# Fifteen of sixteen expert pairs written out, and a loop for the last pair and the overflow

## The chip, the core and the metric

The kernel runs on one core of a Trainium2 chip. A core has five engines, each with its own instruction queue: TensorE (PE, matmuls; its weight loads are shown apart as PEld), VectorE (DVE), ScalarE (ACT), GpSimd (POOL) and SyncE (SP), which here only issues DMAs. Engines wait for each other through semaphores. The metric is the time of one execution on the device in microseconds. The kernel before takes 1500.24 us (median of three runs, 1499.53 to 1501.92).

## What is computed

Two layers of a decoder trunk over 256 positions of width 1024, all in float32. Each layer mixes tokens in three branches and then sends each position through two of 32 experts:

```python
for l in range(DEPTH):                       # DEPTH = 2
    h = rms_norm(x, norm_mix_g[l])
    x = x + token_mixers(h, ...)             # "mixing": one wide projection, three branches, gates, w_out
    h = rms_norm(x, norm_ffn_g[l])
    x = x + hier_moe(h, ...)                 # group (argmax of 4), then top 2 of the 8 experts inside it
return rms_norm(x, norm_final_g)

def expert_block(tok_b, e):                  # inside hier_moe, for the rows of one expert
    xb = xt[tok_b]
    hid = silu(xb @ w_gate[e]) * (xb @ w_up[e])
    return hid @ w_down[e]                   # 1024 -> 512 -> 1024, then weighted and added back to x
```

An expert has three matrices of 2 MB. All 32 are read in each layer, whatever the routing says: 201 MB a layer.

## The kernel before

**Stages.** A layer is a mixing stage (its weights come through a ring of buffers and are split into a high and a low part by ACT and DVE), a short routing stage and an expert stage. The code of both layers is written out in Python, so each layer has its own instructions.

**Expert stage.** Experts are taken two at a time, a pair: experts 2i and 2i+1, each with up to 64 rows (`BLK`), fill the 128 rows of a tile. `MAIN_PAIRS` is 16. An expert with more than 64 rows continues in overflow pairs that follow the sixteen; there can be up to four (`MAX_PAIRS` 20). With these inputs there is none: each layer runs 16 pairs. The number of pairs up to the end of each layer is computed on DVE (L1098 to L1105) and written to `pairs_i`; each queue waits for semaphore `pairs_known` and reads it into a register.

**Weights.** `ring` has 12 slots of 1 MB. A pair uses all twelve: slots 0 to 3 for the first halves of gate and up (two experts each), 4 to 7 for their second halves, 8 to 11 for down. SP's `load_pair` issues them in that order; before each two slots it waits for `pair_freed`, which PE raises after each of the six stages of the pair before (four of `gate_up`, L1455, two of `down`, L1467). The loads of the next layer's mixing weights stand behind them in SP's queue.

**One pair g.** PE's `pair` (L1485) does, in this order: `gate_up` 0; adding rows back for the pair before (`scatter`, L1481/L1482) in two parts around `gate_up` 1; transposes of the selection matrix (L1496, L1498); `gate_up` 2 and 3; `gather(0)` (L1443), the first half of the row gather for pair g+1; transposes of `hid` (L1509), which wait for DVE; `gather(1)`; `down` 0 and 1, which wait for ACT's copy of the transposed `hid` (L735). ACT copies the selection (L730, L731), computes silu (L733), copies `hidT` (L735) and the high part of y (L738). DVE adds rows to x (`add_rows`, L1118), builds the selection of the next pair (`choose`, L1087, L1089), multiplies silu by up (L1128), scales the gathered rows of the next pair (`gathered`, L1111) and computes the low part of y (L1132).

**Start of a stage.** DVE chooses the rows of pair 0, computes the pair count, copies the gathered rows, chooses for pair 1, computes `overflow_tables` (L1139 to L1158) and then finishes pair 0 with L1128. PE gathers for pair 0, reads the pair count, runs pair 0 and then loops over the others. The last trip of the loop also gathers, for a pair that may not exist.

Of the kernel before, what the change touches and what calls it, by code (L numbers as in the profile page):

```python
# [29 lines left out]
P = 128  # L30
ALU = mybir.AluOpType
ACT = mybir.ActivationFunctionType
AX = mybir.AxisListType
# [17 lines left out]
def build_trunk(nc, x_in, positions, norm_mix_g, norm_ffn_g, norm_final_g, w_in, gmlp_ws, gmlp_b, conv_w,  # L51
                w_proj_a, w_proj_b, w_proj_c, w_out, router_group_w, router_group_b,
                router_expert_w, router_expert_b, expert_w_gate, expert_w_up, expert_w_down, out):
    _, S, D = x_in.shape
# [15 lines left out]
    BLK = 64  # L70
# [71 lines left out]
    with ExitStack() as ctx:  # L142
# [265 lines left out]
        def alone(eng):  # L408

            eng.sem_inc(passed)  # L410
# [17 lines left out]
        def sync_program(sp):  # L428
# [6 lines left out]
            for l in range(DEPTH):  # L435

                if_known = l * 1 + 1
                sp.wait_ge(pairs_known, if_known)
                alone(sp)
                done = sp.value_load(pairs_i[0:1, bass.ds(l, 1)], min_val=0, max_val=DEPTH * MAX_PAIRS)  # L440
# [66 lines left out]
                end = sp.value_load(pairs_i[0:1, bass.ds(l + 1, 1)], min_val=MAIN_PAIRS, max_val=DEPTH * MAX_PAIRS)  # L507
# [63 lines left out]
        def scalar_program(act):  # L571
# [168 lines left out]
            act.wait_ge(pairs_known, DEPTH + 1)  # L740
            last = act.value_load(pairs_i[0:1, DEPTH:DEPTH + 1], min_val=MAIN_PAIRS, max_val=DEPTH * MAX_PAIRS)
            sqrt_table()
            act.wait_ge(x_added, last * 2)
# [5 lines left out]
        def vector_program(dve):  # L749
# [48 lines left out]
            for l in range(DEPTH):  # L798
# [283 lines left out]
                def choose(i, g):  # L1082
# [14 lines left out]
                nb = S // BLK - 1  # L1097
                link(v.tensor_tensor(beyond[:, :, :], psD[:, 0, 2 * NE:3 * NE].unsqueeze(2).to_broadcast([P, NE, nb]),  # L1098
                                     thresholds[:, :].unsqueeze(1).to_broadcast([P, NE, nb]), ALU.is_gt))
                link(v.tensor_reduce(cumA[:, 16:], beyond[:, :, :], AX.X, ALU.add))  # L1100
                link(v.tensor_reduce(total[:, :], cumA[:, 16:], AX.X, ALU.add))
# [93 lines left out]
        def tensor_program(pe):  # L1195
# [6 lines left out]
            for l in range(DEPTH):  # L1202
# [321 lines left out]
                with pe.Fori(done + 1, end) as g:  # L1524
                    pair(g, False)
# [46 lines left out]
```

## Time and profile before

| | |
|---|---|
| median of 3 runs | 1500.24 us (1499.53 to 1501.92) |
| the profiled execution | 1495.47 us |
| its span, first to last instruction | 1493.7 us |
| PE busy | 1421.6 us, 95% |
| DVE busy | 557.0 us, 37% |
| ACT busy | 423.5 us, 28% |
| weight loads (queue q1) | 488.20 MB, 81.6% of 16 DMA engines' span |
| instruction queues q8 and q14 | 27 and 12 packets, 0.44 and 0.10 MB |
| mean granted clock of TensorE | 0.983 |

A slice of the span is 37.3 us. The mixing stages take about 0 to 265 and 745 to 1003 us, the expert stages 276 to 747 and 1014 to 1485 us. Busy time alone does not tell what bounds: PE is counted busy while a matmul is in the array, and in the expert stages the weight stream is as full as PE is. Times of pieces come from this one profiled execution.

### The profile page before, as it was taken

The page shows a single profiled execution, that of the slowest core. Times are in us where ns is not written, and L with a number is a line of the kernel's source. Part 1 is how long each engine was busy: PE and PEld are TensorE (multiplying, and loading weights), DVE is VectorE, ACT ScalarE, POOL GpSimd, SP SyncE. Part 2 cuts the span into 40 slices and gives each one's busy share as a digit, 9 for nine tenths or more (in the row PEclk, how much of TensorE's full clock was granted, in tenths as well). Part 3 has the DMA queues.
Part 4 walks back from the last instruction along what each step waited for, and adds up shares of the span by engine and source line. Part 5 has one row for each costly group of instructions (what it writes and reads, how often), then busy time and mean ns, then how long its engine had stood idle before and what let it go on. Part 6 is the DMA issues. An engine that isn't in the chain of part 4 may idle for free.

```text
span 1493.7 us, 19746 instructions
## 1 busy us (share of the span) xinstructions
PE 1421.6 (95%) x7463; PEld 859.2 (58%) x7463; DVE 557.0 (37%) x871; ACT 423.5 (28%) x530; POOL 7.5 (0%) x43
## 2 busy tenths in 40 slices
PE   6999999899999999999989999998999999999996
PEld 5899788544444444444478988874444444444443
DVE  6786355522222222212277844654222222222123
ACT  5544332312212212111254543431221221221121
POOL 1000000000000000000000000000000000000000
PEclk9999899899999999999989999998999999999999
DMA  7544364899999999999945443748999999999995
GB/s 271 184 162 169 127 214 165 328 416 422 422 422 422 422 421 422 422 422 423 408 172 177 149 165 137 253 153 359 420 422 422 422 422 422 422 422 422 421 422 229
DMA packets 100799, 489.08 MB, mean 327 GB/s; under 512 B 8686, under 2 KB 12054, under 8 KB 51608
## 3 DMA queue, kind: packets, MB, share of 16 engines
q1 hardware_dynamic: 99656, 488.20, 81.6%
q8 instruction: 27, 0.44, 0.1%
q10 hardware_dynamic: 1104, 0.34, 0.1%
q14 instruction: 12, 0.10, 0.0%
HBM read 487.46 MB, written 1.05 MB: 327 GB/s over the span
## 4 chain that ended last, share of the span: by engine, by line
PE 65%; DMA 24%; DVE 8%; issue 2%; ACT 1%; SPq 0%; POOL 0%; DVEq 0%; ACTq 0%; POOLq 0%
DMA ring<-in_expert_w_up_dram 24%; PE psB L1455 19%; PE psA L1219 14%; PE psB L1219 11%; PE psC L1467 8%; PE psA L1443 5%; DVE ring_parts L814 2%; PE psA L1481 2%; PE psA L1482 1%; DVE work L909 1%; DVE top L908 1%; PE psD L1509 1%; PE psC L1341 1%; PE psC L1340 1%; PE psC L1424 1%
## 5 line engine op out<-in xcount | busy, mean ns | idle before, releaser
L1455 PE MATMUL psB<-ring,share 128*64 128x512 f32 x2048 | 462.5, 596 | 17.9 <-DMA ring<-in_expert_w_up_dram 17.9
L1455 PEld LDWEIGHTS psB<-ring,share 128*64 128x64 f32 x2048 | 142.0, 137 | 290.5 <-issue 270.7
L1467 PE MATMUL psC<-ring,share 128*64 128x512 f32 x1024 | 226.8, 595 | 0.0
L814 DVE TENSOR_TENSOR ring_parts<-ring,ring_parts 128x2048 fp32r<-128x2048 f32 (+1 forms) x80 | 176.7, 2248 | 64.7 <-ACT ring_parts L637 64.4
L637 ACT ACTIVATE ring_parts<-ring 128x2048 fp32r<-128x2048 f32 (+1 forms) x80 | 146.9, 1878 | 57.9 <-PE psA L1219 38.3
L1118 DVE TENSOR_TENSOR x<-x,psA 128x1024 f32<-128x1024 f32 x62 | 75.7, 1221 | 191.4 <-PE psA L1482 191.4
L1467 PEld LDWEIGHTS psC<-ring,share 128*64 128x64 f32 x1024 | 70.8, 137 | 131.7 <-issue 127.8
L1443 PEld LDWEIGHTS psA<-gates,xn 128*128 128x128 f32 x1088 | 130.1, 196 | 27.7 <-issue 26.0
L1443 PE MATMUL psA<-gates,xn 128*128 128x128 f32 x1088 | 139.0, 282 | 1.6 <-DVE gates L1087 1.6
L1219 PE MATMUL psA<-ring_parts,hT_parts 128*128 128x512 f32 (+1 forms) x448 | 134.8, 383 | 2.0 <-DVE ring_parts L847 2.0
L1132 DVE TENSOR_TENSOR gates_parts<-psC,gates_parts 128x512 fp32r<-128x512 f32 x64 | 41.2, 685 | 222.8 <-ACT gates_parts L738 222.8
L1219 PE MATMUL psB<-ring_parts,hT_parts 128*128 128x512 f32 x384 | 121.6, 398 | 0.0
L738 ACT ACTIVATE gates_parts<-psC 128x512 fp32r<-128x512 f32 x64 | 34.7, 595 | 262.9 <-PE psC L1467 262.9
L1219 PE MATMUL psA<-ring_parts 128*128 128x512 f32 (+2 forms) x320 | 109.2, 341 | 0.0
L1219 PE MATMUL psB<-ring_parts 128*128 128x512 f32 (+1 forms) x288 | 99.7, 346 | 0.0
L1128 DVE SCALAR_TENSOR_TENSOR share<-gates,psB 128x512 f32<-128x512 f32 x32 | 23.9, 747 | 197.5 <-PE psB L1455 197.0
L1219 PEld LDWEIGHTS psA<-ring_parts,hT_parts 128*128 128x128 f32 x448 | 83.7, 191 | 17.3 <-issue 2.7
L1219 PEld LDWEIGHTS psB<-ring_parts,hT_parts 128*128 128x128 f32 x384 | 73.4, 193 | 16.2 <-issue 1.1
L1111 DVE TENSOR_TENSOR share<-psA,g_ffn 128x512 f32<-128x512 f32 x68 | 47.0, 691 | 94.7 <-PE psA L1443 94.7
L730 ACT ACTIVATE gates<-psD 64x1 f32<-64x1 f32 x64 | 10.6, 165 | 247.8 <-PE psD L1498 247.4
L735 ACT ACTIVATE share<-psD 128x512 f32<-128x512 f32 x32 | 19.1, 597 | 189.8 <-PE psD L1509 189.8
L1219 PEld LDWEIGHTS psA<-ring_parts 128*128 128x128 f32 x320 | 61.3, 192 | 6.2
(313 smaller groups left out, 1237.3 us busy)
## 6 DMA issues: line engine op xcount, KB each, us to landing
ring<-in_expert_w_gate_dram SPq DMA_DIRECT2D x128, 1024.0 KB, 19.9
ring<-in_expert_w_up_dram SPq DMA_DIRECT2D x128, 1024.0 KB, 20.9
ring<-in_expert_w_down_dram SPq DMA_DIRECT2D x128, 1024.0 KB, 19.5
ring<-in_w_in_dram SPq DMA_DIRECT2D x56, 1024.0 KB, 7.1
ring<-in_w_out_dram SPq DMA_DIRECT2D x8, 1024.0 KB, 5.2
ring<-in_w_proj_a_dram SPq DMA_DIRECT2D x4, 1024.0 KB, 6.2
ring<-in_w_proj_b_dram SPq DMA_DIRECT2D x4, 1024.0 KB, 6.2
ring<-in_w_proj_c_dram SPq DMA_DIRECT2D x4, 1024.0 KB, 6.2
```

What stands on the lines that cost most here:

```text
L637: sc.activation(high_and_low(p)[0], mix_slot(p), ACT.Copy).then_inc(high_act, 1)
L738: sc.activation(y_high[:, n, :], psC[:, n, :], ACT.Copy).then_inc(y_act, 1)
L814: v.tensor_tensor(low_part, mix_slot(p), high_part, ALU.subtract).then_inc(low_dve, 1)
L1111: v.tensor_tensor(xT[:, 4 * b:4 * b + 4, :], psA[:, b, :].rearrange("p (c n) -> p c n", c=4), g_ffn[:, 4 * b:4 * b + 4].unsqueeze(2).to_br ...
L1118: v.tensor_tensor(x[:, t, :].rearrange("p (b n) -> p b n", b=2), x[:, t, :].rearrange("p (b n) -> p b n", b=2), (psB if last and t else ps ...
L1128: v.scalar_tensor_tensor(hid, silu, slot_w, psB[:, 1, :], ALU.mult, ALU.mult).then_inc(hid_done, 1)
L1132: v.tensor_tensor(y_low[:, n, :], psC[:, n, :], y_high[:, n, :], ALU.subtract).then_inc(y_dve, 1)
L1219: ins = te.matmul(o, first, second, start=start and i == 0, stop=stop and i == len(TERMS) - 1)
L1443: ins = te.matmul(psA[:, b, (c % 4) * P:(c % 4 + 1) * P], xn[:, o:o + P], sel[:, t].rearrange("p j n -> p (j n)"), start=t == 0, stop=t == ...
L1455: ins = te.matmul(psB[j * BLK:(j + 1) * BLK, o, :], xT[:, 4 * half + c, j * BLK:(j + 1) * BLK], w[:, c, :], start=half == 0 and c == 0, st ...
L1467: ins = te.matmul(psC[j * BLK:(j + 1) * BLK, n, :], hidT[:, 2 * k + c, j * BLK:(j + 1) * BLK], w[:, c, n * 512:(n + 1) * 512], start=k == ...
L1481: te.matmul(ps[:, n, :], selT[:, t, :], y_high[:, n, :], start=True, stop=False)
```

## The change

Per engine:

- PE: fifteen pairs are written out. Each gathers for the next, except the last of the fifteen (pair 14). Then PE reads the pair count, and a loop covers pair 15 and any overflow pair; each trip gathers its own rows first, both halves, and then runs `pair` without a gather.
- DVE: the same fifteen are written out. The seven instructions of the pair count (`pair_count`) move from before the first `gathered` to after `choose_next(0)`, in front of `overflow_tables`. In the loop a trip copies its own gathered rows, adds the rows of the pair before, chooses for the next and finishes its pair.
- ACT: fifteen trips written out, then the count is read and a loop covers the rest.
- SP keeps its loop. All four queues no longer read the count at the head of a layer: layer 0 counts from the constant 0, layer 1 from the register that holds the end of layer 0.

The arithmetic, the weight loads and their order stay the same. The diff, cut to its core:

```diff
@@ SP, head of a layer
-                if_known = l * 1 + 1
-                sp.wait_ge(pairs_known, if_known)
-                alone(sp)
-                done = sp.value_load(pairs_i[0:1, bass.ds(l, 1)], min_val=0, max_val=DEPTH * MAX_PAIRS)
+                done = end if l else 0
@@ ACT
-                act.wait_ge(pairs_known, l + 1)
-                alone(act)
-                start = act.value_load(pairs_i[0:1, bass.ds(l, 1)], min_val=0, max_val=DEPTH * MAX_PAIRS)
+                start = end if l else 0
...
-                act.wait_ge(pairs_known, l + 2)
-                alone(act)
-                end = act.value_load(pairs_i[0:1, bass.ds(l + 1, 1)], min_val=MAIN_PAIRS, max_val=DEPTH * MAX_PAIRS)
-                with act.Fori(start, end) as g:
+                def pair(g):
...
+                for i in range(MAIN_PAIRS - 1):
+                    pair(start + i)
+                act.wait_ge(pairs_known, l + 2)
+                alone(act)
+                end = act.value_load(pairs_i[0:1, bass.ds(l + 1, 1)], min_val=(l + 1) * MAIN_PAIRS, max_val=(l + 1) * MAX_PAIRS)
+                with act.Fori(start + MAIN_PAIRS - 1, end) as g:
+                    pair(g)
@@ DVE
-                dve.wait_ge(pairs_known, l + 1)
-                alone(dve)
-                start = dve.value_load(pairs_i[0:1, bass.ds(l, 1)], min_val=0, max_val=DEPTH * MAX_PAIRS)
+                start = end if l else 0
...
-                nb = S // BLK - 1
-                link(v.tensor_tensor(beyond[:, :, :], psD[:, 0, 2 * NE:3 * NE].unsqueeze(2).to_broadcast([P, NE, nb]),
...
-                v.tensor_copy(pairs_i[:, bass.ds(l + 1, 1)], pairs_f[:, :]).then_inc(pairs_known, 1)
...
-                        dve.wait_ge(gather_ps, (g + l) * 2 + b + 1)
+                        dve.wait_ge(gather_ps, g * 2 + b + 1)
...
-                def pair_rest(g):
+                def pair_rest(g, gather_next):
...
-                    gathered(g + 1)
+                    if gather_next:
+                        gathered(g + 1)
...
-                gathered(start)
-                choose_next(0, start)
-                overflow_tables()
-                pair_rest(start)
-                with dve.Fori(0, nc.s_assert_within(end - start - 1, MAIN_PAIRS - 1, MAX_PAIRS - 1)) as i:
-
-                    add_rows(start + i)
-                    choose_next(i + 1, start + i + 1)
-                    pair_rest(start + i + 1)
+                gathered(start)
+                choose_next(0, start)
+                pair_count()
+                overflow_tables()
+                pair_rest(start, True)
+                for i in range(1, MAIN_PAIRS - 1):
+                    add_rows(start + i - 1)
+                    choose_next(i, start + i)
+                    pair_rest(start + i, i < MAIN_PAIRS - 2)
+                dve.wait_ge(pairs_known, l + 2)
+                alone(dve)
+                end = dve.value_load(pairs_i[0:1, bass.ds(l + 1, 1)], min_val=(l + 1) * MAIN_PAIRS, max_val=(l + 1) * MAX_PAIRS)
+                with dve.Fori(0, nc.s_assert_within(end - start - (MAIN_PAIRS - 1), 1, MAX_PAIRS - MAIN_PAIRS + 1)) as i:
+
+                    gathered(start + i + MAIN_PAIRS - 1)
+                    add_rows(start + i + MAIN_PAIRS - 2)
+                    choose_next(i + MAIN_PAIRS - 1, start + i + MAIN_PAIRS - 1)
+                    pair_rest(start + i + MAIN_PAIRS - 1, False)
@@ PE
-                pe.wait_ge(pairs_known, l + 1)
-                alone(pe)
-                done = pe.value_load(pairs_i[0:1, bass.ds(l, 1)], min_val=0, max_val=DEPTH * MAX_PAIRS)
+                done = end if l else 0
...
-                    pe.wait_ge(sel_ready, g + l + 2)
-                    pe.wait_ge(x_added, g * 2 + 1)
-                    gather(0)
+                    if gather_next:
+                        pe.wait_ge(sel_ready, g + l + 2)
+                        pe.wait_ge(x_added, g * 2 + 1)
+                        gather(0)
...
-                    gather(1)
+                    if gather_next:
+                        gather(1)
...
+                for i in range(MAIN_PAIRS - 1):
+                    pair(done + i, i == 0, i < MAIN_PAIRS - 2)
...
-                pair(done, True)
-                with pe.Fori(done + 1, end) as g:
-                    pair(g, False)
+                end = pe.value_load(pairs_i[0:1, bass.ds(l + 1, 1)], min_val=(l + 1) * MAIN_PAIRS, max_val=(l + 1) * MAX_PAIRS)
+                with pe.Fori(done + MAIN_PAIRS - 1, end) as g:
+
+                    pe.wait_ge(sel_ready, g + l + 1)
+                    pe.wait_ge(x_added, g * 2 - 1)
+                    gather(0)
+                    gather(1)
+                    pair(g, False, False)
```

## Rows read from the trace of the kernel before

**Rows 1.** The page: busy totals, and GB/s moved in 40 slices of the span.

```profile
PE 1421.6 (95%) x7463; PEld 859.2 (58%) x7463; DVE 557.0 (37%) x871; ACT 423.5 (28%) x530; POOL 7.5 (0%) x43
...
GB/s 271 184 162 169 127 214 165 328 416 422 422 422 422 422 421 422 422 422 423 408 172 177 149 165 137 253 153 359 420 422 422 422 422 422 422 422 422 421 422 229
```

**Rows 2.** Chain in order of time (start us, us, what): pair 1, PE.

```profile
308.75 3.43 PE psB L1455 x16
313.31 3.58 PE psB L1455 x16
318.58 7.02 PE psB L1455 x32
```

**Rows 3.** The same chain, the end of the first layer's expert stage.

```profile
702.14 25.39 DMA ring<-in_expert_w_up_dram
...
727.66 3.65 PE psB L1455 x16
731.32 1.98 PE psA L1443 x16
733.30 0.48 PE psD L1509 x4
733.78 1.79 PE psA L1443 x16
735.57 7.04 PE psC L1467 x32
```

**Rows 4.** ACT reads the count (ns min/median/max, starts); first table load after it.

```profile
L586 ACTq TENSOR_LOAD <-pairs_i x2: 275/380/486, 7.1 to 742.9; - x2
...
7.85 1.28 ACT L581 ACT_TABLE_LOAD   x1 [0.49 <-issue]
```

**Rows 5.** Timeline of pair 0 (start us, us, engine, line; in brackets idle time before).

```profile
276.00 0.25 DVE L1098 TENSOR_TENSOR ycT<-psD,thresholds 128x96 f32<-128x96 f32 x1
277.44 0.15 DVE L1105 CAST pairs_i<-pairs_f 128x1 int32<-128x1 f32 x1
...
279.89 0.69 DVE L1111 TENSOR_TENSOR share<-psA,g_ffn 128x512 f32<-128x512 f32 x1 [2.29 <-PE psA L1443]
...
297.69 0.49 DVE L1158 TENSOR_REDUCE ycT<-rel 128x10 f32<-128x320 f32 x1
298.40 0.75 DVE L1128 SCALAR_TENSOR_TENSOR share<-gates,psB 128x512 f32<-128x512 f32 x1 [0.22 <-DVE ycT L1158]
299.20 0.75 PE L1509 MATMUL psD<-ident,share 128*128 128x128 f32 x4 [0.76 <-DVE share L1128]
299.99 0.60 ACT L735 ACTIVATE share<-psD 128x512 f32<-128x512 f32 x1 [6.31 <-PE psD L1509]
```

**Rows 6.** SP's down loads; windows; landings of loads issued 304.5 to 307, 284 to 287.

```profile
305.49 4.27 SPq L446 DMA_DIRECT2D ring<-in_expert_w_down_dram  x4
...
307.00:308.00 1.00, 1.00 (x8) 0.30 (x6) 0.00 (x0) 0.00 (x0) 0.00 (x0) 1.00 0.87 336
308.00:309.00 1.00, 1.00 (x6) 0.29 (x4) 0.00 (x0) 0.20 (x1) 0.00 (x0) 1.00 1.01 369
309.00:310.00 1.00, 1.00 (x8) 0.42 (x6) 0.57 (x1) 0.98 (x3) 0.00 (x0) 1.00 0.92 385
...
ring<-in_expert_w_down_dram SPq DMA_DIRECT2D x2, 1024.0 KB, 7.8
...
ring<-in_expert_w_gate_dram SPq DMA_DIRECT2D x2, 1024.0 KB, 6.1
```

**Rows 7.** PE from 400 to 700 us; instruction packets of the span, of 310:500, of 295:298.

```profile
400.00:700.00 300.00, 292.15 (x1503) 132.50 (x1501) 64.39 (x93) 58.18 (x95) 0.00 (x0) 1.00 1.01 422
...
q8 instruction: 27, 0.44, 0.1%
...
q8 instruction: 1, 0.02, 0.0%
...
q8 instruction: 1, 0.02, 2.1%
```

More of the change, by code:

```diff
@@ L506, in sync_program @@
                 alone(sp)
-                end = sp.value_load(pairs_i[0:1, bass.ds(l + 1, 1)], min_val=MAIN_PAIRS, max_val=DEPTH * MAX_PAIRS)
+                end = sp.value_load(pairs_i[0:1, bass.ds(l + 1, 1)], min_val=(l + 1) * MAIN_PAIRS, max_val=(l + 1) * MAX_PAIRS)
                 with sp.If(end > done + MAIN_PAIRS):
@@ L738, in scalar_program @@
                         sc.activation(y_high[:, n, :], psC[:, n, :], ACT.Copy).then_inc(y_act, 1)
-            act.wait_ge(pairs_known, DEPTH + 1)
-            last = act.value_load(pairs_i[0:1, DEPTH:DEPTH + 1], min_val=MAIN_PAIRS, max_val=DEPTH * MAX_PAIRS)
+                for i in range(MAIN_PAIRS - 1):
[5 more added lines that the diff above has]
+                    pair(g)
             sqrt_table()
-            act.wait_ge(x_added, last * 2)
+            act.wait_ge(x_added, end * 2)
             sc.activation(xn[:, 0:D], x[:, 0, :], ACT.Square, accum_out=ss[:, 0:1]).then_inc(ss_act, 1)
@@ L1132, in pair_rest, with pair_count @@
                         v.tensor_tensor(y_low[:, n, :], psC[:, n, :], y_high[:, n, :], ALU.subtract).then_inc(y_dve, 1)
+                def pair_count():
+                    nb = S // BLK - 1
+                    link(v.tensor_tensor(beyond[:, :, :], psD[:, 0, 2 * NE:3 * NE].unsqueeze(2).to_broadcast([P, NE, nb]),
+                                         thresholds[:, :].unsqueeze(1).to_broadcast([P, NE, nb]), ALU.is_gt))
+                    link(v.tensor_reduce(cumA[:, 16:], beyond[:, :, :], AX.X, ALU.add))
+                    link(v.tensor_reduce(total[:, :], cumA[:, 16:], AX.X, ALU.add))
+                    link(v.tensor_scalar(npair[:, :], bidx[:, 0:OVER_BLOCKS:QB], total[:, 0:1], None, ALU.is_lt))
+                    link(v.tensor_reduce(total[:, :], npair[:, :], AX.X, ALU.add))
+                    link(v.scalar_tensor_tensor(pairs_f[:, :], total[:, :], float(MAIN_PAIRS), pairs_f[:, :], ALU.add, ALU.add))
+                    v.tensor_copy(pairs_i[:, bass.ds(l + 1, 1)], pairs_f[:, :]).then_inc(pairs_known, 1)
                 def overflow_tables():
@@ L1483, in scatter, with pair @@
                     ins.then_inc(scatter_ps[t], 1)
-                def pair(g, first):
-                    pe.wait_ge(xT_done, (g + l) * 2 + 1)
+                def pair(g, first, gather_next):
+                    pe.wait_ge(xT_done, g * 2 + 1)
                     gate_up(g, 0)
-                    pe.wait_ge(xT_done, (g + l) * 2 + 2)
+                    pe.wait_ge(xT_done, g * 2 + 2)
                     if not first:
@@ L1519, in tensor_program @@
                 gather(1)
+                for i in range(MAIN_PAIRS - 1):
+                    pair(done + i, i == 0, i < MAIN_PAIRS - 2)
                 pe.wait_ge(pairs_known, l + 2)
                 alone(pe)
-                end = pe.value_load(pairs_i[0:1, bass.ds(l + 1, 1)], min_val=MAIN_PAIRS, max_val=DEPTH * MAX_PAIRS)
-                pair(done, True)
-                with pe.Fori(done + 1, end) as g:
-                    pair(g, False)
+                end = pe.value_load(pairs_i[0:1, bass.ds(l + 1, 1)], min_val=(l + 1) * MAIN_PAIRS, max_val=(l + 1) * MAX_PAIRS)
[5 more added lines that the diff above has]
+                    pair(g, False, False)
                 for t in range(NT):
```

7 lines of the change are left out of this document (removed).

## The prediction

> **What bounds the kernel now.** I read the slices of the span first, then the chain of work in order of time, then its pieces at the two ends of an expert stage. The slices show two expert stages with the weight stream flat at 422 GB/s, and PE is busy 95% of the span [rows 1]. The chain tells which of the two ends last. In the first pairs of a stage it runs from matmul to matmul: one pair takes 28.1 us of PE (from the gate and up products at 308.75 to the next at 336.9, the sum of the pieces of which three stand in [rows 2]). From the tenth pair on it is load, matmul, load: 25.4 us from the issue of an up-projection load to its landing, 3.7 us of matmuls that free the slot, and again, 29.82 us a pair [rows 3]. A pair carries twelve loads of 1.049 MB, and 12.6 MB at 422 GB/s is the same 29.8 us. So PE first works off the slots that were full when the stage began, catches up with the stream, and from then on the stream sets the pace. A stage ends when its last weights have landed and PE has done what depends on them. What branches, register loads or waits cost on PE, ACT and DVE in the middle is covered by the 29.8 - 28.1 = 1.7 us a pair that PE has to spare. The change counts in four places only: the first pair, the stream itself, the last two pairs, the launch.
>
> **Part 1: the loop control that goes.** Per layer each of the four queues drops one read of the pair count (0.3 to 0.5 us on ACT, the two in [rows 4]). On PE in the first pair it runs while the gathers are still in the array, and the gate products follow them without a gap, so its removal is worth nothing. The read at the head of layer 1 lies under the last y copies, that of DVE in the mixing stage under a wait for PE. Only at launch is one on the path: ACT's at 7.1 us holds back the square-root table load, which starts at 7.85 us [rows 4]. About 0.5 us is freed there, half of it is then DVE's own norm: -0.2 us, bounds -0.5 and 0. What SP drops waits at launch for the credits of GpSimd anyway: 0. The branches of fifteen trips cost nothing by the 1.7 us of cover; without that cover they would be some tenths of a microsecond a trip.
>
> **Part 2: the count of pairs, moved.** Its seven DVE instructions ran from 276.00 to 277.59 us, beside PE's first gathers, where DVE had 2 us to wait anyhow [rows 5]. Now they stand between the second choice of rows and the overflow tables, in front of the first pair's product of silu and up. There DVE is already late: the tables end at 298.18, the product starts at 298.40, and PE has idled 0.76 us for it [rows 5]. So 1.5 us goes straight onto PE before the first down projections. ACT's hidT copy and SP's next two loads stand behind it. Does it reach the stream? SP issues the four down loads from 305.49 on as those slots come free [rows 6]. In the microseconds from 307 the stream falls to 336, 369 and 385 GB/s, 0.4 us of it lost [rows 6]: the queue is dry just when these loads come, so a later issue seems lost one for one, +1.5 us a layer. Against it: the first pair of these loads takes 7.8 us to land, one issued onto an idle queue 6.1 us [rows 6]; 1.5 + 6.1 is 7.6, so a load issued 1.5 us later onto a dry queue would land no later. Bounds 0 and +1.5 us; both rows are of this very spot, and I take the middle, +0.8 us a layer.
>
> **Part 3: fifteen pairs as straight code.** This is the edit with a price on the resource that bounds. A pair is 1503 matmuls in 300 us [rows 7], so 149 of them at 29.8 us a pair, and as many weight loads: 298. Before, a layer holds two such bodies and repeats the second; after, it holds sixteen. The larger instruction queue moves packets of 16 KB, 27 in the span, but only one between 310 and 500 us [rows 7]: the loop body was fetched once and stayed. Of the 2 x 7463 matmuls and weight loads [rows 1] 28 x 298 are repeats, so 27 packets carried some 6580 distinct ones, 244 each; fourteen bodies more are 17 packets more a layer, one every 26 us. One packet between 295 and 298 us took 2.1% of 16 engines, which is 1.0 us of one engine [rows 7], an engine that otherwise carries weights at its full rate. A load is cut over all 16 engines and lands with the slowest. Bounds: spread evenly, 17 x 1.0 / 16 = 1.1 us a layer; all on one engine, 17 us. No row names the engine. Weight traffic is spread evenly, and I lean to that end: with 17 packets on 16 engines the unluckiest takes two, so +2.0 us a layer, the few small packets of DVE and ACT included. The Trainium skill (Runtime: NRT & Kernel Launch, Instruction fetch mechanics) says that code is streamed in 16 KB blocks of 256 instructions and that crossing a block is mostly hidden. By that sentence this term would be 0 and the total that of the first rival; the block size agrees with the trace, and hidden for the engine that runs the code need not be hidden for a saturated stream.
>
> **Part 4: the last two pairs.** Pair 14 (counted from 0) no longer gathers for pair 15. Before, the stretch from the end of the gate and up products to the down products was 1.98 + 0.48 + 1.79 us of PE, 4.25 us in all, the gathers covering DVE's product and ACT's copy [rows 3]. Without them these stand bare: 0.75 us of DVE, 0.75 of PE, 0.60 of ACT [rows 5] and the semaphores, 2.3 us. So pair 14's down products start 2.0 us sooner, but their second half then waits for its weights: four loads of 2.49 us behind the up loads that landed 29.8 us before 727.5 [rows 3], at 707.6. They end at 711.4 instead of 712.7. Pair 15 then gathers its rows in front, 3.8 us (1.98 + 1.79), and DVE's first copy of them (0.7 us) hides under the second gather. What is queued behind on DVE is the addition of pair 14's rows, which PE wants only after its first gate product. Its gate products start at 715.2; 4.6 + 5.3 + 7.0 us [rows 2] lead to 732.1, no load being later than that (the last up load lands at 727.5 [rows 3]). Bare stretch 2.3: down products at 734.4, their last weights at 727.5 + 4 x 2.49 = 737.5, end at 741.4. Before: 735.57 + 7.04 = 742.6 [rows 3]. So -1.2 us a layer; at best -1.4 (the landing is the limit), at worst +0.1 if entering the loop costs its read of the count and a branch on DVE and PE in the open and code arrives late. I take -1.1. The next layer's weight loads are issued up to 2 us later, but the stream still has work until 737.5: nothing.
>
> **Sum.** Per layer 0.8 + 2.0 - 1.1 = +1.7 us, twice +3.4, launch -0.2: +3.2 us. On the profiled execution of 1495.5 us (span 1493.7) that gives 1498.7. The median of the timed runs stands 4.8 us above it, and I carry that over: 1503.4 us. A measurement of this kernel can tell 0.2%, 3.0 us, from no change; so the forecast lies on the edge of that.
>
> **Rivals.** First, the code costs the stream nothing and the dry queue swallows the moved count: 2 x (-1.1) - 0.2 = -2.4 us, 1497.8. For it: the 6.1 us landing, and that fetches went on all through the mixing stage unnoticed. Against it: 1.0 us on an engine that has none to spare. It decides from the point where the slowest engine at the end of a stage is one that had no extra packet. With all bounds at their best (-1.4 twice, -0.5) it is -3.3, 1496.9, just below the edge. Second, the packets go to few engines: on four, 17 x 1.0 / 4 = 4.3 us a layer instead of 2.0, +7.8 us in all, 1508; on one, +33 us, 1533. Nothing on the page names the engine. Third, nothing moves: the removed control was hidden and parts 2 to 4 cancel, 1500 to 1501.5; the second layer still counts from a register, so only half of the fifteen pairs' arithmetic becomes constant. The skill's same section also says that a taken branch to code that is not resident stalls its engine. By it the removed loops would give time back; the quiet queue between 310 and 500 us shows that the body was resident, so I give it no more than the best end of the first rival.
>
> **How the numbers follow.** Forecast (1501.5 to 1506) 0.40, of which 0.30 is over 1503.2; first rival 0.30 (0.08 below 1497.2); second 0.15; third 0.10; anything else, such as a clock step that falls elsewhere, 0.05, mostly small. Faster by over 0.2% 0.10, within 0.45, slower 0.45. The range goes from 1497.2 to 1510: it leaves out the best end of the first rival and the heavier half of the second, under 2 in 10.
>
> **What would show it.** Right: more 16 KB instruction packets in the expert stages, one every 26 us or so; the wait of PE for DVE in the first pair at 2.3 us instead of 0.76; the first down loads issued 1.5 us later, counted from the stage's first gather; a hidT stretch of 2.3 us in pairs 14 and 15; a span of the load-bound pairs above 29.82 us. Wrong: load-bound pairs that stay at 29.82 us and a stage that ends no later (the first rival), or pairs at 30.1 us and more (the second). A PE that no longer catches up with the stream, or waits for code, would overturn the whole account.

## The result and the profile after

The changed kernel takes 1507.61 us (median of six runs, 1498.46 to 1507.86); the kernel before, on the same chip, 1499.88 us (1497.22 to 1501.92). The ratio is 1.0047, 95% interval [1.0031, 1.0063]: 7.0 us slower by the ratio, 7.7 us between the medians, more than the 0.2% that a measurement can tell. The forecast was 1503.4 us within 1497.2 to 1510.

The page of the changed kernel, to be held against [rows 1] and [rows 7]: its span, its busy totals, the GB/s in 40 slices and the two instruction queues (packets, MB, share of 16 engines); then the larger queue in the window from 310 to 500 us alone.

```profile
span 1496.7 us, 18955 instructions
...
PE 1413.8 (94%) x7399; PEld 852.9 (57%) x7399; DVE 554.4 (37%) x867; ACT 344.0 (23%) x468; POOL 7.5 (0%) x43
...
GB/s 271 188 157 169 163 219 132 364 407 421 420 421 421 421 421 421 421 420 422 404 146 176 170 168 132 235 177 347 416 421 421 420 421 421 421 421 421 421 421 224
...
q8 instruction: 59, 0.97, 0.3%
...
q14 instruction: 17, 0.14, 0.0%
```

```profile
q8 instruction: 8, 0.13, 0.3%
```

PE, DVE and ACT all have less work and the kernel is slower. What moved against it is small: 59 instead of 27 packets of code, eight instead of one between 310 and 500 us, and weight slices of 420 and 421 GB/s where 422 stood.

The profiled execution took 1498.46 us, only 3.0 us above that of before, and here a reader must look at where the two differ before taking 3.0 for the cost. I divided both traces into four stretches, by the start of PE's first gate product of each expert stage and the end of its last down product (worked out from the records of PE):

| us | before | after | difference |
|---|---|---|---|
| start to expert stage 0 | 281.65 | 278.09 | -3.6 |
| expert stage 0 | 460.94 | 463.87 | +2.9 |
| between the stages | 276.77 | 276.79 | 0.0 |
| expert stage 1 | 460.38 | 464.00 | +3.6 |

Of the -3.6 us only 0.4 us, at launch, are the change's (see the last sections). For the rest: in both kernels the granted clock falls to 0.50 (the 1.2 GHz level) in the middle of the first mixing stage; in the profile of before from 153.6 us for 10.2 us, in this one from 156.4 us for 3.4 us. 6.8 us less at half the clock give back 3.4 us. In the twelve profiles of this case the stretch in this place lasts 3.4, 6.8 or 10.2 us, whatever the kernel, and the five other runs of the changed kernel had a mean clock of 0.978 to 0.980, the profiled one 0.986. So the cost is that of the expert stages: 2.9 + 3.6 = 6.5 us, close to what the timed runs show.

**The first pair.** Timeline of layer 0 (start us, us, engine, line; in brackets the idle time before):

```profile
295.64 0.49 DVE L1156 TENSOR_REDUCE ycT<-rel 128x10 f32<-128x320 f32 x1
296.17 0.75 DVE L1114 SCALAR_TENSOR_TENSOR share<-gates,psB 128x512 f32<-128x512 f32 x1
...
296.97 0.75 PE L1511 MATMUL psD<-ident,share 128*128 128x128 f32 x4 [2.08 <-DVE share L1114]
```

PE's wait for DVE went from 0.76 us [rows 5] to 2.08. The pair, from the first gate product to the first down product, takes 21.34 us instead of 20.02. The next view is of the weight stream where SP issues the four down loads of that pair, at 303.26 us, which is 25.17 us into the stage; before it was 305.49 [rows 6], 23.84 us into it. The last column is GB/s:

```profile
302.00:303.00 1.00, 1.00 (x8) 0.37 (x6) 0.00 (x0) 0.00 (x0) 0.00 (x0) 1.00 1.02 426
303.00:304.00 1.00, 1.00 (x8) 0.35 (x6) 0.00 (x0) 0.00 (x0) 0.00 (x0) 1.00 0.57 238
304.00:305.00 1.00, 1.00 (x6) 0.29 (x4) 0.00 (x0) 0.00 (x0) 0.00 (x0) 1.00 0.91 164
305.00:306.00 1.00, 1.00 (x8) 0.36 (x6) 0.00 (x0) 0.00 (x0) 0.00 (x0) 1.00 0.81 254
306.00:307.00 1.00, 1.00 (x8) 0.35 (x6) 0.00 (x0) 0.43 (x1) 0.00 (x0) 1.00 0.97 410
```

Against 422 GB/s the three dips are short of 184 + 258 + 168 = 610, or 1.45 us of stream. Before, the three of [rows 6] are short of 86 + 53 + 37 = 176, or 0.42 us. So 1.03 of the 1.33 us by which the loads were later is lost to the stream. In layer 1 the same sum, over all windows from 20 to 40 us into the stage, is 0.4 us before and 2.2 us after (1.5 in the second profile of this kernel).

**The end of the stage.** The chain in order of time (start us, us, what), to be held against [rows 3], and PE's timeline of the last pair:

```profile
675.03 7.04 PE psC L1468 x32
...
682.71 24.13 DMA ring<-in_expert_w_down_dram
...
706.98 3.67 PE psC L1468 x16
...
711.30 26.87 DMA ring<-in_expert_w_down_dram
...
738.31 3.67 PE psC L1468 x16
```

```profile
732.76 0.75 PE L1511 MATMUL psD<-ident,share 128*128 128x128 f32 x4 [0.84 <-DVE share L1114]
734.20 3.65 PE L1468 MATMUL psC<-ring,share 128*64 128x512 f32 x16 [0.69 <-ACT share L727]
738.31 3.65 PE L1468 MATMUL psC<-ring,share 128*64 128x512 f32 x16 [0.46 <-DMA ring<-in_expert_w_down_dram]
```

The stage now ends with a load: PE waits for the last down weights in pair 14 (706.98) and in pair 15 (738.31). The stretch without gathers takes 731.92 to 734.20, 2.28 us; the forecast had 2.3. From the last landing to the end of the stage it is 3.8 us in both layers, where before it was 5.1: PE's part became 1.3 us shorter. But the last landing itself came later: 460.08 and 460.21 us into the stages instead of 455.89 and 455.28. The whole loss is in the stream.

**Where the stream lost it.** A load of 1 MB is carried by 16 DMA engines, and the trace has the moment at which each reports its part. These are the 16 moments of one load about 440 us into stage 0, in us behind the first engine, sorted (worked out from those records, not a view of the profile):

```
before            0 .1 .2 .3 .5 .6 .7 .7 .8 .9 .9 1.2 1.3 1.5 2.1 2.3
after             0 .1 .2 .2 .3 .4 1.1 1.6 3.1 3.4 3.5 3.5 3.6 3.7 3.9 4.0
```

Half of the engines are 3 to 4 us behind the others, and the load lands with them; at the stage's last load the slowest is 5.5 us behind. The lag is built up in steps. The loads that land at 316.1 and 318.6 us have their slowest engine 0.9 us behind; one 16 KB packet of code starts at 320.38 and takes 1.15 us; the load that lands at 322.6 has its slowest engine 2.4 us behind, the next ones 2.3. And it lasts: 200 us into the stage no engine is over 2.4 us behind, at 300 us four are, at 400 eight, at 440 eight.

The same reading can be made at every later packet. Counted from the one at 320 us, there are sixteen packets in the first 440 us of the stage, and with nearly every one a single engine falls back by 1.5 to 1.6 us against the others: first one engine after another until eight have had a step, then, as far as sorted moments can tell, the same eight once more. The packet 441 us into the stage begins a third round: the slowest engine goes from 4.0 to 5.4 us behind. The kernel before has one such packet in this stretch (at 322 us), and it makes one step of 1.55 us, which is most of the 2.3 us in its list.

### The profile page after: what moved, and what is told of

It reads as the page before. It is cut to its first block, busy times and chain, and to the rows that moved or that the text cites. A ratio compares the mean times of both kernels' runs of the same rounds, so it can differ in the third digit from the quotient of the medians.

```text
span 1496.7 us, 18955 instructions
## 1 busy us (share of the span) xinstructions
PE 1413.8 (94%) x7399; PEld 852.9 (57%) x7399; DVE 554.4 (37%) x867; ACT 344.0 (23%) x468; POOL 7.5 (0%) x43
## 4 chain that ended last, share of the span: by engine, by line
PE 64%; DMA 24%; DVE 8%; issue 2%; ACT 1%; SPq 0%; POOL 0%; DVEq 0%; POOLq 0%
DMA ring<-in_expert_w_up_dram 19%; PE psB L1456 19%; PE psA L1220 14%; PE psB L1220 11%; PE psC L1468 9%; DMA ring<-in_expert_w_down_dram 5%; PE psA L1444 5%; DVE ring_parts L812 2%; PE psA L1482 2%; PE psA L1483 1%; DVE work L907 1%; DVE top L906 1%; PE psD L1511 1%; PE psC L1425 1%; PE psC L1342 0%
## 5 line engine op out<-in xcount | busy, mean ns | idle before, releaser
L1456 PE MATMUL psB<-ring,share 128*64 128x512 f32 x2048 | 462.5, 596 | 18.7 <-DMA ring<-in_expert_w_up_dram 16.2
L1444 PEld LDWEIGHTS psA<-gates,xn 128*128 128x128 f32 x1024 | 122.0, 196 | 26.2 <-issue 25.3
L1444 PE MATMUL psA<-gates,xn 128*128 128x128 f32 x1024 | 130.1, 282 | 1.6 <-DVE gates L1083 1.6
```

The lines of the kernel that those rows point to most:

```text
L1444: ins = te.matmul(psA[:, b, (c % 4) * P:(c % 4 + 1) * P], xn[:, o:o + P], sel[:, t].rearrange("p j n -> p (j n)"), start=t == 0, stop=t == ...
L1456: ins = te.matmul(psB[j * BLK:(j + 1) * BLK, o, :], xT[:, 4 * half + c, j * BLK:(j + 1) * BLK], w[:, c, :], start=half == 0 and c == 0, st ...
```

## The experiments

All ten kernels were timed in five rounds beside the kernel before (its median 1499.1 to 1499.5 us in these comparisons). Three properties are varied: the straight code, the late pair count, and the missing gather in pair 14. This table has them all; the stage columns are layer 0 / layer 1 in us, "lag" is slowest behind fastest engine at the stage's last load in us, "late engines" counts those over 2.4 us behind at 440 us of stage 0, "packets" are those of q8.

| kernel | PE code | count | gather | ratio [95%] | stage | lag | late engines | packets |
|---|---|---|---|---|---|---|---|---|
| before | loop | early | kept | 1 | 460.94 / 460.38 | 2.38 / 2.02 | 0 | 27 |
| after | straight | late | gone | 1.0047 [1.0031, 1.0063] | 463.87 / 464.00 | 5.52 / 5.20 | 8 | 59 |
| after_again | straight | late | gone | 1.0044 [1.0029, 1.0060] | 463.19 / 463.19 | 4.76 / 4.58 | 8 | 59 |
| straight | straight | early | kept | 1.0045 [1.0030, 1.0060] | 464.58 / 463.28 | 6.28 / 4.75 | 8 | 60 |
| countback | straight | early | gone | 1.0021 [1.0009, 1.0033] | 462.40 / 462.65 | 5.42 / 5.09 | 8 | 59 |
| gather_as_before | straight | late | kept | 1.0050 [1.0033, 1.0067] | 466.66 / 466.19 | 5.47 / 4.67 | 8 | 60 |
| loop15 | loop | late | gone | 1.0019 [1.0010, 1.0028] | 462.18 / 462.53 | 2.18 / 1.97 | 0 | 31 |
| lastpairs | loop | early | gone | 0.9985 [0.9975, 0.9996] | 459.68 / 459.70 | 2.24 / 2.15 | 0 | 31 |
| pe_looped | loop | late | gone | 1.0007 [0.9995, 1.0019] | 462.66 / 462.50 | 2.50 / 2.50 | 1 | 31 |
| pe_straight | straight | late | gone | 1.0048 [1.0033, 1.0062] | 464.41 / 464.69 | 4.51 / 4.77 | 8 | 59 |
| poolcode | loop | early | kept | 1.0266 [1.0247, 1.0285] | 481.90 / 481.44 | 18.09 / 18.04 | 1 | 27 |
| split_tables | loop | early | gone | 0.9966 [0.9952, 0.9979] | 459.51 / 459.37 | 2.09 / 2.24 | 0 | 31 |

### The changed kernel once more

> The changed kernel once more, for a second profile and the state of TensorE's clock beside it. In its first profile the two expert stages (first gate product to the end of the last down product) take 463.9 and 464.0 us, against 460.9 and 460.4 before; the timed runs are 7.7 us above, the profiled span only 3.0 us. Theory: the stages stay at +3 to +4 us each in every execution, and what is left of the difference is one stretch at half clock in the middle of a mixing stage, which lasts 3.4 us in some executions and 10.2 us in others. Rival: the stages themselves differ from execution to execution by several us, because other DMA engines are hit by the instruction packets. Theory gives about 1503 to 1508, stages 464 again.

1505.27 us, ratio 1.0044. Its own profile has a span of 1505.7 us, at a clock of 0.977: without the lucky mixing stage of the first profile the span is where the timed runs are. Its stages cost +2.25 and +2.8 us, below the +3 to +4 expected: two profiles of one kernel, with the same 59 packets and the same eight late engines, have stages that differ by 0.7 and 0.8 us, and the differences between single profiles below are no finer than that. So the slowdown repeats (1.0044 beside 1.0047), and the profiled +3.0 us was the accident.

### One part at a time: the straight code

The first kernel of this group takes the straight code out and leaves the rest.

> The changed kernel with its code folded again: pairs 1 to 13 run in a loop on PE, DVE and ACT, pairs 0 and 14 are written out on PE and DVE; the moved count, the dropped reads and the last two pairs stay. If straight code costs the weight stream (theory: 3 us a layer at the end of the stage), the stages fall from 464 to about 461 us, below or near the kernel before, and the time to about 1500 (6 us less than the changed kernel); the packets of PE's instruction queue fall from 59 to about 31. If the code costs nothing and the loss is the moved count alone, the stages stay at 463 to 464 and the time does not move.

```diff
 # PE, and ACT and DVE in the same manner
-for i in range(MAIN_PAIRS - 1):
-    pair(done + i, i == 0, i < MAIN_PAIRS - 2)
+pair(done, True, True)
+with pe.Fori(done + 1, done + MAIN_PAIRS - 2) as g:
+    pair(g, False, True)
+pair(done + MAIN_PAIRS - 2, False, False)
```

1501.39 us, ratio 1.0019. The lag is back at 2.2 and 2.0 us and no engine is late, with 31 packets. The stages, 462.2 and 462.5 us, are above the 461 expected: in the first pair it has a clock stretch that the profiles of the changed kernel lack (more on that below). The next one keeps the straight code alone.

> Straight code alone: fifteen pairs written out, but each pair gathers for the next, the last trip too, as before, and the count is in its old place. If straight code is the cost, the stages are 3 us longer than before (464) and the time is 6 us above it (1506); the packets of PE's instruction queue are about 60. If the loss came from the moved count or the entry of the loop, this kernel is at the time of before (1500).

```diff
+pair_count()
 gathered(start)
 choose_next(0, start)
-pair_count()
...
-    pair_rest(start + i, i < MAIN_PAIRS - 2)
+    pair_rest(start + i, True)
...
-    gathered(start + i + MAIN_PAIRS - 1)       # head of a trip of the last loop; PE in the same manner
```

1505.02 us, ratio 1.0045: straight code alone makes nearly the whole loss, +3.6 and +2.9 us of stage. The first pair (19.82 us) is as short as before and the end behind the last landing (5.0 and 5.1 us) is as long; only the landings are late, by the lag.

### Is it the code, and on which engines?

The lag could still have come from something else in the new order. So this kernel is the one before, untouched, with nothing but more code: GpSimd, which is idle in the expert stages, runs 300 semaphore increments a pair that nobody waits for.

> The kernel before, with GpSimd, which has nothing to do in the expert stages, stepping through 300 plain semaphore increments after the gate products of each of fifteen pairs: 9000 instructions of straight code in all, about as many as PE gets more by the change, on an engine that nobody waits for. Theory (fetched code delays single DMA engines of the saturated weight stream): both stages get longer, from 460.9 and 460.4 to about 463 us, the time rises by 4 to 6 us to about 1504, and the small instruction packets rise by about 70. Rival (what costs is how PE, ACT or DVE run their own straight code): stages at 461 and the time of before, 1499.

```diff
+for i in range(MAIN_PAIRS - 1):                                     # GpSimd, per layer
+    pool.wait_ge(pair_freed, (l * MAIN_PAIRS + i + 1) * STAGES + 3)
+    for _ in range(300):
+        pool.sem_inc(filler)
```

```profile
span 1536.6 us, 28746 instructions
...
q8 instruction: 27, 0.44, 0.1%
...
q14 instruction: 83, 0.68, 0.1%
```

```profile
659.83 26.66 DMA ring<-in_expert_w_up_dram
...
690.95 26.64 DMA ring<-in_expert_w_up_dram
```

1539.32 us, 40 us slower, where 4 to 6 us were expected, by 9000 instructions on an engine that nobody waits for. The direction held; the expectation had the size wrong by a factor of eight or so, because it did not foresee where the packets go. The page shows 71 more packets of 8 KB, 0.58 MB among 488 MB, at 0.1% of the engines' time. The chain shows load-bound pairs of 31.1 us (690.95 - 659.83) where before they were 29.82 us [rows 3]. The landings say why:

```
poolcode, 440 us of stage 0: fifteen engines within .7 us, the sixteenth 17.5 us behind
```

The packets of this queue put back one DMA engine only. Between 30 and 438 us of a stage there are 31 of them, each busy for 0.31 us, and each but the first two adds 0.6 to 0.7 us to the lag of that one engine. At the stage's last load the lag is 15.7 us more than before (18.1 against 2.4); the rest of the stage's 21 us is that even the fastest engine's part lands later (by 5.2 us; that slots come free later would do it, and was not shown). The page counts the packets' time as a share of sixteen engines, while a load lands with its slowest. This shows that fetched code delays weights by itself, and how: by what it puts on the fullest engine. (The same increments in a short loop, without the code, were not run; that the lag grows packet by packet speaks against the increments themselves.) It does not show whose packets make the steps in the changed kernel; the next two do.

> The changed kernel with one edit: PE's pairs 1 to 13 of a layer run in a loop again; those of DVE and ACT stay written out. Theory (the lag of the slowest DMA engine, 5 to 6 us at the end of a stage, comes from PE's 16 KB instruction packets): packets of the larger instruction queue back to about 31, lag back to 2.0 to 2.6 us, expert stages about 460.5 to 461 us (462.5 where the clock step falls into the first pair), ratio to the kernel before about 1.0015. Rival (the smaller packets of DVE and ACT do it): packets back to about 31 but the lag stays at 5 us and more, stages stay at 463 to 464 us, ratio 1.004 to 1.005.

```diff
 # the changed kernel; ACT and DVE stay written out
-for i in range(MAIN_PAIRS - 1):                 # PE
-    pair(done + i, i == 0, i < MAIN_PAIRS - 2)
+pair(done, True, True)
+with pe.Fori(done + 1, done + MAIN_PAIRS - 2) as g:
+    pair(g, False, True)
+pair(done + MAIN_PAIRS - 2, False, False)
```

> The changed kernel with the mirror edit: PE's fifteen pairs stay written out; ACT's and DVE's (pairs 1 to 13) run in loops again. Theory (PE's packets): about 59 packets of the larger instruction queue, lag 5 to 6 us, expert stages 463 to 464 us, ratio 1.004 to 1.005. Rival (DVE's and ACT's packets): lag 2.0 to 2.6 us, stages 460.5 to 461 us, ratio about 1.0015.

```diff
 # the changed kernel; PE stays written out
-for i in range(MAIN_PAIRS - 1):                 # ACT; DVE in the same manner
-    pair(start + i)
+with act.Fori(start, start + MAIN_PAIRS - 1) as g:
+    pair(g)
```

The queue q8 of the two, first that with PE looped:

```profile
q8 instruction: 31, 0.51, 0.1%
```

```profile
q8 instruction: 59, 0.97, 0.3%
```

With PE looped 1500.92 us and a lag of 2.5 us; with PE straight 1506.59 us, eight late engines and a lag of 4.5 to 4.8 us, somewhat below the 5 to 6 expected, and stages of 464.4 and 464.7 us, somewhat above the 463 to 464 expected. The ratios, 1.0007 and 1.0048, have intervals far apart. The 16 KB packets are PE's and they are the cost. ACT's and DVE's written-out code costs nothing that can be told: pe_looped has it and loop15 does not, and pe_looped's stages are 0.5 us longer in layer 0 and equal in layer 1, its ratio even lower.

The size follows too. By the steps watched above the slowest engine of the changed kernel has taken three packets when the last load lands, and the slowest engine before had taken one. Two more at 1.55 us are 3.1 us, and the lags differ by 3.1 and 3.2 us; the straight code alone measured +3.6 and +2.9 us of stage.

### The moved count, and the clock

> The changed kernel with only the seven DVE instructions of the pair count back in their old place, ahead of the first copy of gathered rows. If a later first down load is lost to the dry stream, both stages get 1 to 1.5 us shorter and the time falls by 2 to 3 us (about 1504). If the idle queue swallows it, the wait of PE for DVE in the first pair goes back from 2.1 to 0.76 us and the time stays within 1 us.

```diff
+pair_count()
 gathered(start)
 choose_next(0, start)
-pair_count()
 overflow_tables()
```

Timeline of pair 0 of this kernel:

```profile
297.60 0.75 PE L1511 MATMUL psD<-ident,share 128*128 128x128 f32 x4 [0.56 <-DVE share L1114]
```

1500.94 us, ratio 1.0021. The wait is 0.56 us instead of 2.08, and the stages are 1.47 and 1.35 us shorter than those of the changed kernel. Against the second profile of the changed kernel the stages are 0.8 and 0.5 us shorter. The timed runs put the whole move at 3.9 us (1.0047 against 1.0021; 3.4 us by after_again), with some 3 us of uncertainty. So the move costs time, about 1.4 us a layer; how much exactly is not settled.

It can be more. In the four experiments that have the late count and are not the changed kernel itself (loop15, gather_as_before, pe_looped, pe_straight) the clock fell in the first pair of both layers, eight of eight stages. One of them, pe_looped, first PE's timeline and then the windows around it, where the third column from the right is the granted clock:

```profile
301.04 0.98 PE L1511 MATMUL psD<-ident,share 128*128 128x128 f32 x4 [2.09 <-DVE share L1114]
```

```profile
300.00:301.00 1.00, 0.00 (x0) 0.00 (x0) 0.96 (x3) 0.00 (x0) 0.00 (x0) 1.00 0.97 410
301.00:302.00 1.00, 0.96 (x5) 0.96 (x6) 0.58 (x1) 0.00 (x0) 0.00 (x0) 0.69 0.99 418
302.00:303.00 1.00, 1.00 (x7) 1.00 (x6) 0.00 (x0) 0.60 (x1) 0.00 (x0) 0.50 1.06 442
303.00:304.00 1.00, 1.00 (x7) 1.00 (x7) 0.00 (x0) 0.00 (x0) 0.00 (x0) 0.50 1.01 426
304.00:305.00 1.00, 1.00 (x7) 0.99 (x6) 0.00 (x0) 0.00 (x0) 0.00 (x0) 0.61 0.96 401
```

PE stands idle for 2.09 us, and then 3.4 us run at the half clock, which makes the first pair 22.8 to 23.1 us instead of 21.4. In the four stages of the changed kernel that were profiled, with the same idle time, the clock stayed at 1.00; and no kernel with the early count, whose idle time there is 0.8 us or less, has such a stretch in pair 0. So this idle time goes along with the stretch but does not force it. Whether the unprofiled runs of the changed kernel had it is open.

What the late stretch costs at the end of a stage these profiles do not settle. It puts 1.5 us on the first pair, and pe_straight's last landing is 0.5 and 0.7 us later than that of the changed kernel's first profile, but 1.2 and 1.5 us later than that of its second.

### The last two pairs

> The changed kernel with every pair gathering for the next again, the last trip too; straight code and the moved count stay. If the last two pairs give back 1.2 us a layer in the changed kernel, the stages here are 465.2 us and the time is 2 to 2.5 us above it (about 1508). If the extra packets at the end of a stage already cover that, the stages stay at 464.

```diff
-    pair_rest(start + i, i < MAIN_PAIRS - 2)
+    pair_rest(start + i, True)
...
-    gathered(start + i + MAIN_PAIRS - 1)       # head of a trip of the last loop; PE in the same manner
```

1506.69 us, ratio 1.0050: the count and the straight code without the gain of the last pairs. The time was expected 2 to 2.5 us above the changed kernel's; by the ratios it is 0.5 us above, which the intervals cannot tell from either. Its stages are 2.2 to 2.8 us longer than the changed kernel's, with the clock stretch in them that the other lacks; against pe_straight, which has it too, they are 2.25 and 1.5 us longer. The cleaner measure is the next kernel, which has this part alone.

> The kernel before with only two parts of the change: the last pair in its own loop, gathering its rows first, and the dropped reads; pairs 1 to 13 in a loop, the count in its old place. Theory: the last two pairs give 1.2 us a layer, stages 459.7 and 459.2, time 1496 to 1497. If the entry of the loop eats the gain, as at the worst end of the prediction, stages 461 and the time of before.

It is loop15 and countback together: loops on all engines, the count early, pair 14 without a gather. Its chain at the end of stage 0:

```profile
683.26 24.05 DMA ring<-in_expert_w_down_dram
...
707.45 3.65 PE psC L1471 x16
711.10 3.77 PE psA L1447 x32
714.87 3.58 PE psB L1459 x16
...
734.17 7.11 PE psC L1471 x32
```

1497.20 us, ratio 0.9985 [0.9975, 0.9996]: faster than the kernel before. The stages are 1.26 and 0.68 us shorter than before, where 1.2 was expected of both. Nearly every term of the forecast's part 4 can be read off this chain: the down weights land and start their products at 707.45 (worked out 707.6), the products end at 711.10 (711.4), the gate products start at 714.87 (715.2), the last down products at 734.17 (734.4) and end at 741.28 (741.4).

### The better kernel

DVE's wait in pair 0 was 0.76 us before the change, and behind it stood the 0.42 us dip in the stream. The overflow tables in front of it serve only pairs after the sixteenth, so the second of their two iterations can run after DVE's product of silu and up.

> As lastpairs, and the second position tile of the overflow tables is computed after the first pair's product of silu and up, under the down products, so that PE's wait for DVE in the first pair (0.76 us before) goes. Theory: 0.5 to 0.8 us a layer below lastpairs, about 1495. If the stream's restart hides that wait, no gain against lastpairs.

```diff
 # lastpairs, and (overflow_tables keeps its first part; its loop over two tiles becomes overflow_table):
 overflow_tables()
-pair_rest(start, True)
+overflow_table(0)
+pair_rest(start, True, between=lambda: overflow_table(1))   # run between gathered(1) and the low part of y
```

Timeline of pair 0 (DVE, PE), and the windows behind the issue of the down loads at 304.37 us:

```profile
296.49 0.75 DVE L1114 SCALAR_TENSOR_TENSOR share<-gates,psB 128x512 f32<-128x512 f32 x1 [0.59 <-PE psB L1462]
...
298.19 0.64 PE L1517 MATMUL psD<-ident,share 128*128 128x128 f32 x4
```

```profile
307.00:308.00 1.00, 1.00 (x8) 0.39 (x6) 0.00 (x0) 0.32 (x1) 0.00 (x0) 1.00 1.01 418
308.00:309.00 1.00, 1.00 (x8) 0.33 (x6) 0.62 (x2) 0.98 (x3) 0.00 (x0) 1.00 1.02 426
309.00:310.00 1.00, 1.00 (x6) 0.29 (x4) 0.67 (x2) 1.00 (x1) 0.00 (x0) 1.00 1.03 426
```

1494.20 us, ratio 0.9966 [0.9952, 0.9979]: 5 us faster than the kernel before and 12 us faster than the changed one. (The 12 us are by the ratios.) DVE now waits for PE, PE's transposes follow its gathers without a gap, the first pair takes 18.99 us instead of lastpairs' 19.8 and 20.0, and the dip in the stream is gone. But the stages are only 0.2 and 0.3 us shorter than those of lastpairs, where 0.5 to 0.8 were expected: little of what the first pair gained reaches the last landing. Against the kernel before, the stages account for 1.4 + 1.0 = 2.4 of the 5 us, the launch for 0.4; for the rest the traces show nothing but other clock stretches in the mixing stages, so I leave it open, and with it how much of the 2.8 us between this kernel and lastpairs is the split's.

## Why the prediction came out as it did

The direction of the sum was right and the range holds the time. The size was not: +3.2 us forecast, +7 found, outside the band of 1501.5 to 1506 that I gave the likeliest case. Step by step, in us a layer:

| step | forecast | bounds | measured |
|---|---|---|---|
| straight code on the stream | +2.0 | 1.1 to 17 | +3.6 / +2.9 (straight against before) |
| moved count | +0.8 | 0 to 1.5 | +1.5 / +1.4 (after against countback; after_again: +0.8 / +0.5) |
| last two pairs | -1.1 | -1.4 to +0.1 | -1.3 / -0.7 (lastpairs against before) |
| launch, once | -0.2 | -0.5 to 0 | -0.4 |

**The straight code is the step that failed in size.** The mechanism, the number of packets and the place were right: one every 24 us (8 in 190 us) where I had one every 26, 32 more in all where I had 34. Mis-sized was what a packet costs its engine. I reckoned two on the unluckiest of sixteen engines, at the 1.0 us that a packet itself is busy [rows 7]; each put its engine back by 1.5 to 1.6 us. The two came out right by luck: the packets fell in rounds on eight engines and not evenly on sixteen, the slowest engine took three, and before it had already taken one that my sum did not count. 2 x 1.55 is 3.1, between my 2.0 and the second rival's 4.3 (four engines), which had the mechanism and a chance of 0.15. Of the rule of the Trainium skill that crossing a block of code is mostly hidden (Runtime: NRT & Kernel Launch, Instruction fetch mechanics) the traces bear out only one side. PE did not wait for its code: all of its longer waits in stage 0 of the changed kernel, 14.9 us in sum, were for loads (9.8 us), for DVE and for ACT. The stream paid.

**The moved count: I took the middle of two bounds that had an answer.** My argument for zero was that a load issued later onto a dry queue lands sooner, 6.1 us instead of 7.8 [rows 6]. As far as it goes that came true. The same two loads of the changed kernel, those issued from 302 to 304.6 us:

```profile
ring<-in_expert_w_down_dram SPq DMA_DIRECT2D x2, 1024.0 KB, 6.4
```

They take 6.4 us and land no later in layer 0, 30.6 and 33.0 us into the stage where before it was 30.7 and 33.1. But that is the moment of the slowest engine, which for the first load was 1.5 us behind the mean of the sixteen before and is 0.6 us behind it now. Taken over the sixteen engines the first load's parts land 0.9 and 1.0 us later, and the windows show the same: with the loads 1.33 us later, 1.03 us more of the stream is lost. A single load's time from issue to landing was the wrong measure; the sum of missing GB/s over the dip, which [rows 6] already gave as 0.4 us, was the one to trust. It said that engines were already running dry, and then most of a further delay is lost.

**The last two pairs** came out as worked in layer 0 (lastpairs: 741.28 against 741.4 us for the end; layer 1 gained only 0.7 us), with the late landing of pair 14's second down half as the limit. Entering the loop cost nothing that shows: the second gather of pair 15 ends at 714.34 in the changed kernel and its gate products start there.

**The launch.** ACT's second table load starts 0.47 us earlier than in [rows 4], and PE's first transposes, which started at 13.36 us before, 0.42 us earlier. Timeline of ACT and of PE:

```profile
7.38 1.28 ACT L578 ACT_TABLE_LOAD   x1
...
12.94 1.94 PE L1245 MATMUL psA<-ident,xn 128*128 128x128 f32 x8 [4.55 <-ACT xn L599]
```

So what was freed on ACT arrives nearly whole; I had put half of it down to DVE's own work.

**What the median carried.** I put 4.8 us between the profiled execution and the median, as before. For the changed kernel they are 9.1 us apart, because its profiled execution was the one with the short clock stretch in mixing. That does not touch the terms of the sum, but a reader who sets 1498.46 beside 1495.47 gets half the cost.

**The first rival** is refuted in both of its conditions: the code is not free and the dry queue swallows little. What is left of it is its gain, 2 x (-1.1) - 0.2, which lastpairs reached on its own (-2.2 us by its ratio).

Added up, the measured steps of the table give 3.6 + 2.9 + 1.5 + 1.4 - 1.3 - 0.7 - 0.4 = 7.0 us, the measured ratio's; as each comes from single profiles, such a close fit is partly luck.

Still open: why PE's packets fall on eight engines and GpSimd's on one; why a packet costs its engine more than the time that it is busy (1.55 against about 1.1 us, 0.65 against 0.31); and whether the timed runs of the changed kernel had the clock stretch in pair 0.

## What to carry to other kernels

When the DMA stream bounds a stage, instructions are part of the traffic: keep the body of the loop resident and count the packets of the instruction queues, on idle engines too, as time of the fullest DMA engine and not as a share of sixteen. Before moving small work into the first pair of such a stage, look at whether the stream dips there; a dip means that DMA engines run dry, and most of a further delay is lost (here 1.0 of 1.3 us). And compare two profiles stage by stage, since clock stretches elsewhere can be as large as the change.

## What the runs showed that I had not expected

**ACT reloads its function tables in every trip of the long loop.** The fall of ACT's busy time from 423.5 to 344.0 us was in none of my steps. The two large groups of table loads of the kernel before (count; busy us, mean ns; idle before):

```profile
L730 ACT ACT_TABLE_LOAD x32 | 41.1, 1283 | 10.3 <-DVE pairs_i L1105 9.8
L733 ACT ACT_TABLE_LOAD x32 | 41.1, 1283 | 0.6
```

In the changed kernel the first group (the selection) is gone and the second (silu) is left with two:

```profile
L725 ACT ACT_TABLE_LOAD x2 | 2.6, 1283 | 0.0
```

The loop over sixteen pairs loads both tables in each trip. The written-out pairs load the silu table once a layer, at the first silu, and never go back; 62 loads fewer, times 1.283 us, is the 79.5 us. Not every loop does it: the short one around pair 15 adds no load in the changed kernel, and in loop15 each group has 30 loads, not 32. What decides it no run here shows. The loads were hidden: even in the first pair ACT waits 1.56 us for PE after the second load. A kernel that is bound by ACT would gain it.

**Code for an idle engine can be dear.** 9000 instructions on GpSimd, 0.58 MB of code, cost 40 us (poolcode), while their packets are 0.1% of the DMA engines' time on the page.
